# Splitting the first attention head and the GLU rows earlier, key blocks from key 0, and 128-row rotary products in a hybrid decoder layer

## What is computed

```python
proj = rmsnorm(h) @ w_in                      # u | z_s | c_q | c_kv | k_pe | z_a
ys = gelu(ssm_scan(u) + d * u)                # S5 heads
ys = ys * sigmoid(ys @ w_glu + b_glu)         # GLU
ssm_out = ys * silu(z_s)                      # 1024 rows of comb
q = rmsnorm(c_q) @ w_uq                       # 8 heads, 128 + 64 (rotary)
c, k_pe = rmsnorm(c_kv), rope(k_pe)
o = attention(q, c, k_pe, causal) @ w_uv      # prompt: per head; sample: over pages
y = concat(ssm_out, o * silu(z_a)) @ w_out    # comb, 2048 rows
out = rmsnorm(h + y)
```

## Time and profile before

| | before |
|---|---|
| median of 3 runs | 1257.17 us (1252.75 to 1259.44) |
| the profiled execution | 1260.12 us |
| its span, first to last instruction | 1258.4 us |
| PE busy | 1128.7 us (90%) |
| PE weight load busy | 1032.3 us (82%) |
| DVE busy | 585.2 us (47%) |
| ACT busy | 375.0 us (30%) |
| POOL busy | 120.8 us (10%) |
| mean granted clock of PE | 0.946 of full speed |

### The profile page before, as it was taken

The page is one execution under the profiler, slowest core; times in us unless marked ns, Lnnn a source line. Parts: engine busy times, 40 slices in busy tenths (PEclk is TensorE's granted clock), DMA queues, the critical chain, the costliest instruction groups (busy, mean ns, idle before and its releaser), DMA issues.

```text
span 1258.4 us, 25162 instructions
## 1 busy us (share of the span) xinstructions
PE 1128.7 (90%) x9906; PEld 1032.3 (82%) x9906; DVE 585.2 (47%) x1205; ACT 375.0 (30%) x622; POOL 120.8 (10%) x192
## 2 busy tenths in 40 slices
PE   3899949999999999596989997799999988999993
PEld 3799949999999999586989975566666648999992
DVE  5843513442588521384646363455555462232224
ACT  6311101111233222335422213444444351121213
POOL 0000110000000000003405301022223100000000
PEclk8799969999999999698989898899999999999996
DMA  9343491332343532415437656166777728323203
GB/s 265 85 126 102 119 145 43 86 85 85 94 125 102 143 103 82 101 47 180 126 92 218 201 179 212 34 194 194 214 213 220 203 76 266 105 67 100 84 17 135
DMA packets 197187, 165.70 MB, mean 132 GB/s; under 512 B 35195, under 2 KB 163478, under 8 KB 195270
## 3 DMA queue, kind: packets, MB, share of 16 engines
q1 hardware_dynamic: 176358, 118.08, 33.4%
q0 software_dynamic: 9696, 27.04, 8.0%
q10 hardware_dynamic: 11048, 19.41, 4.6%
HBM read 139.36 MB, written 22.78 MB: 129 GB/s over the span
## 4 chain that ended last, share of the span: by engine, by line
PE 80%; DVE 6%; DMA 5%; ACT 3%; issue 3%; SPq 1%; POOL 0%; ACTq 0%; DVEq 0%
PE gemm L1758 13%; PE gemm L1760 13%; PE gemm L1759 13%; PE gemm L2084 5%; PE gemm L2086 4%; PE gemm L2085 4%; PE misc L1997 4%; PE gemm L2037 3%; PE gemm L2016 2%; DMA w_raw<-w_out 1%; PE misc L1834 1%; PE misc L1841 1%; PE misc L1983 1%; PE misc L1785 1%; PE gemm L1947 1%
## 5 line engine op out<-in xcount | busy, mean ns | idle before, releaser
L1758 PE MATMUL gemm<-xh,w_hi 128*128 128x260 f32 (+2 forms) x1120 | 321.9, 287 | 0.2 <-DVE w_lo L1152 0.2
L1760 PE MATMUL gemm<-xh,w_lo 128*128 128x260 f32 (+2 forms) x1120 | 319.8, 286 | 0.0
L1759 PE MATMUL gemm<-xl,w_hi 128*128 128x260 f32 (+2 forms) x1120 | 319.5, 285 | 0.0
L1152 DVE TENSOR_TENSOR w_lo<-w_raw,w_hi 128x2048 fp32r<-128x2048 f32 (+3 forms) x65 | 113.6, 1748 | 259.8 <-ACT w_hi L787 258.8
L1758 PEld LDWEIGHTS gemm<-xh,w_hi 128*128 128x128 f32 x1120 | 212.2, 189 | 1.1 <-DVE w_lo L1152 0.4
L1759 PEld LDWEIGHTS gemm<-xl,w_hi 128*128 128x128 f32 x1120 | 212.3, 190 | 0.0
L1760 PEld LDWEIGHTS gemm<-xh,w_lo 128*128 128x128 f32 x1120 | 212.1, 189 | 0.0
L787 ACT ACTIVATE w_hi<-w_raw 128x2048 fp32r<-128x2048 f32 (+3 forms) x63 | 90.7, 1439 | 354.7 <-PE gemm L1760 339.4
L2084 PE MATMUL gemm<-comb_hi,w_hi 128*128 128x260 f32 x512 | 147.4, 288 | 3.9 <-DVE w_lo L1642 2.9
L2086 PE MATMUL gemm<-comb_hi,w_lo 128*128 128x260 f32 x512 | 145.4, 284 | 0.0
L2085 PE MATMUL gemm<-comb_lo,w_hi 128*128 128x260 f32 x512 | 145.4, 284 | 0.0
(11 more groups left out here) (340 smaller groups left out, 1949.1 us busy)
## 6 DMA issues: line engine op xcount, KB each, us to landing
w_raw<-w_in SPq DMA_DIRECT2D x35, 1024.0 KB, 6.0
...
z_d<-ev ACTq DMA_DIRECT2D x16, 260.0 KB, 2.1
...
```

The lines of the kernel that those rows point to most:

```text
L1152: dve.tensor_tensor(w_lo[:, slot, 0:width], w_raw[:, slot, 0:width], w_hi[:, slot, 0:width].bitcast(F32), ALU.subtract).then_inc(w_lo_read ...
L1758: pe.matmul(acc, a, xa, start=k == 0, stop=False)
L1759: pe.matmul(acc, a, xb, start=False, stop=False)
L1760: last = pe.matmul(acc, b, xa, start=False, stop=k == k_tiles - 1)
```

## The change

1. Head 0 is split during the value projection (ACT after v = 7, DVE after v = 8), `kp_lo` after v = 5, and `scores(0)` is made by PE at v = 9, ahead of the last latent transposes. An exponential of one column at v = 5 on ACT asks for its table. SP loads head 1 as soon as head 0 is split; head 1 is split at the end of tile 1. The stores of `kout` stand behind `exponential(0)` and are awaited by SP only at the end.
2. `kp_lo` gets 128 rows, the lower 64 zero.
3. The fourth tile's scores are two halves of 264 keys. Key blocks are counted from key 0, so a tile's diagonal reaches over a block's end by 16 keys of the last 16 queries; these go as a transpose of 32 rows by 16 keys (`EDGE` = 32), and the values' products start `EDGE` columns earlier from the second block on; a memset makes the rest zero.
4. GLU rows are split as they are made: low part into `comb_lo` (in place of `comb`), high part into `ghi`, stored to `g_d` in memory and loaded into `comb_hi[:, 0:8]` near the end of attention.
5. The rows of the heads are split one at a time: head 5 in tile 26, heads 0 to 2 in tile 30, 3, 4 and 6 in tile 31, 7 at the end. `gate_o` of the last head stands ahead of `sample_weights`.
6. `w_out` blocks 2 and 3 are loaded before `yt`; the half of block 1 is cut into 6, 5 and 5 k-tiles.

The diff, without semaphore renames and code that only moves:

```diff
-        EXTRA = slice(496, 512)
-        NM, SM, SME, RS, PARTS = 24, 32, 40, 48, 56
+        HALF = T_PROMPT // 2
+        NM, SM, SME, RS, PARTS, SPARE = 24, 32, 40, 48, 56, 60
+        HEADS_SPLIT = (5, 0, 1, 2, 3, 4, 6, 7)
+        SPLIT_AT = {26: (0,), 30: (1, 2, 3), 31: (4, 5, 6)}
...
-                sp.dma_start(vraw[:, u, 0:4, :], v_d[N_META:T_PROMPT, cols].rearrange("(t p) c -> p t c", p=P)).then_inc(v_loaded[u], 16)
-                sp.dma_start(vraw[0:N_META, u, 4, :], v_d[0:N_META, cols]).then_inc(v_loaded[u], 16)
+                sp.dma_start(vraw[:, u, 0:4, :], v_d[0:4 * P, cols].rearrange("(t p) c -> p t c", p=P)).then_inc(v_loaded[u], 16)
+                sp.dma_start(vraw[0:N_META, u, 4, :], v_d[4 * P:T_PROMPT, cols]).then_inc(v_loaded[u], 16)
...
+            sp.wait_ge(head_lo_done, 1)
+            load_raw(1)
+            load_rotary(1)
             sp.wait_ge(table_loaded, 16)
             sp.wait_ge(v_ready, 10)
             load_group(sp, 3)
...
-            sp.wait_ge(kpe_stored, 16 * 3)
-            sp.wait_ge(head_lo_done, 1)
-            load_raw(1)
-            load_rotary(1)
...
+            sp.wait_ge(opv_done, pages_freed(26))
+            sp.dma_start(comb_hi[:, 0:8, N_META:T].bitcast(F32), g_d.rearrange("(k p) t -> p k t", p=P)[:, :, N_META:T]).then_inc(glu_loaded, 16)
...
+            for u in range(2):
+                sp.wait_ge(w_lo_ready, B_OUT + 1 + u)
+                load_out(2 + u, u)
             sp.wait_ge(ot_ready, 2)
...
-            with sp.Fori(0, 7) as i:
+            with sp.Fori(0, 6) as i:
                 for u in range(2):
-                    sp.wait_ge(w_lo_ready, i * 2 + (B_OUT + 1 + u))
-                    load_out(i * 2 + (2 + u), u)
+                    sp.wait_ge(w_lo_ready, i * 2 + (B_OUT + 3 + u))
+                    load_out(i * 2 + (4 + u), u)
+            sp.wait_ge(kpe_stored, 16 * 3)
+            for u in range(2):
+                sp.wait_ge(glu_stored[u], 16 * 4)
...
+            def keep_high(k):
+
+                act.wait_ge(gated, k + 3)
+                if k < 2:
+                    act.wait_ge(ev_stored[k % 2], 16 * (EV_STORES[k % 2] - 8 + 1))
+                else:
+                    act.wait_ge(comb_lo_done, k - 1)
+                    act.wait_ge(glu_stored[k % 2], 16 * (k // 2))
+                act.activation(ghi[:, k % 2, N_META:T], comb[:, k, N_META:T], ACT.Copy).then_inc(comb_hi_done, 1)
+                act.wait_ge(comb_hi_done, k + 1)
+                act.dma_start(g_d[k * P:(k + 1) * P, N_META:T], ghi[:, k % 2, N_META:T].bitcast(F32)).then_inc(glu_stored[k % 2], 16)
+
...
+                if n > B_GLU:
+                    keep_high(n - B_GLU - 1)
...
+            keep_high(7)
...
+                if v == 5:
+                    act.activation(stat[:, SPARE:SPARE + 1], ident[:, 0:1], ACT.Exp)
+                if v == 7:
+                    head_hi(0)

             act.wait_ge(v_ready, 10)
...
-            head_hi(0)
-            act.wait_ge(kpe_copied, 1)
-            kv = kout[:]
-            act.dma_start(KPE_OUT[0][0:512, :].rearrange("(t p) r -> p t r", p=P), kv[:, 0:4, :]).then_inc(kpe_stored, 16)
-            act.dma_start(KPE_OUT[0][512:T_PROMPT, :], kv[0:N_META, 4, :]).then_inc(kpe_stored, 16)
...
-                    act.activation(out[:, N_META:T_PROMPT], S_BANK[1][:], ACT.Exp, scale=SCALE, bias=bias,
+                    act.activation(out[:, HALF:T_PROMPT], S_BANK[1][:, 0:HALF], ACT.Exp, scale=SCALE, bias=bias,
                                    accum_out=stat[:, SM + at_m:SM + at_m + 1])
-                    act.activation(out[:, 0:N_META], S_BANK[0][:, EXTRA], ACT.Exp, scale=SCALE, bias=bias,
+                    act.activation(out[:, 0:HALF], S_BANK[0][:, 0:HALF], ACT.Exp, scale=SCALE, bias=bias,
                                    accum_out=stat[:, SME + at_m:SME + at_m + 1]).then_inc(exp_done, 1)

...
-                tiles = min(i + 1, 3)
-                act.activation(pt[0:N_META, 0, q], TP[0:N_META, 0:P], ACT.Copy)
-                act.activation(pt[:, 1:1 + tiles, q], TP[:, P:(tiles + 1) * P].rearrange("p (j q) -> p j q", q=P), ACT.Copy).then_inc(pt_copied, 1)
+                last = act.activation(pt[:, 0:i + 1, q], TP[:, 0:(i + 1) * P].rearrange("p (j q) -> p j q", q=P), ACT.Copy)
+                if i < 3:
+                    last = act.activation(pt[0:N_META, i + 1, (i + 1) * P - EDGE:(i + 1) * P], TP[0:N_META, (i + 1) * P:(i + 1) * P + EDGE], ACT.Copy)
+                last.then_inc(pt_copied, 1)

             def copy_last_turned(m):

                 act.wait_ge(pt_ready, rounds(m) + 2)
-                act.activation(pt[:, 4, 3 * P:4 * P], TP[:, 0:P], ACT.Copy).then_inc(pt_copied, 1)
+                act.activation(pt[0:N_META, 4, 4 * P - EDGE:4 * P], TP[0:N_META, 0:EDGE], ACT.Copy).then_inc(pt_copied, 1)
...
+            def comb_high(h):
+                act.wait_ge(o_gated, h + 1)
+                if h < 5:
+                    act.wait_ge(opv_done, pages_freed(27))
+                else:
+                    act.wait_ge(kpe_stored, 16 * 3)
+                act.activation(comb_hi[:, 8 + h, OWN_COLS], comb[:, 8 + h, OWN_COLS], ACT.Copy).then_inc(comb_hi_done, 1)
...
+            act.wait_ge(kpe_copied, 1)
+            kv = kout[:]
+            act.dma_start(KPE_OUT[0][0:512, :].rearrange("(t p) r -> p t r", p=P), kv[:, 0:4, :]).then_inc(kpe_stored, 16)
+            act.dma_start(KPE_OUT[0][512:T_PROMPT, :], kv[0:N_META, 4, :]).then_inc(kpe_stored, 16)
+            act.dma_start(KPE_OUT[1], kv[N_META:N_META + N_SAMPLE, 4, :]).then_inc(kpe_stored, 16)
...
-                    if n // 4 + 1 < N_HEADS:
+                    if n and n // 4 + 1 < N_HEADS:
                         head_hi(n // 4 + 1)
                 copy_turned(n)
                 if n % 4 and n + 1 < N_TILES:
                     exponential(n + 1)
+                if n == 1:
+                    head_hi(1)
...
+                if n in SPLIT_AT:
+                    for i in SPLIT_AT[n]:
+                        comb_high(HEADS_SPLIT[i])
+
             copy_last_turned(N_TILES - 1)
             sample_exp(N_SAMPLE - 1)
-            act.wait_ge(o_gated, 7)
-            for r in (8, 10, 12, 14):
...
+            def keep_low(k):
+                dve.wait_ge(comb_hi_done, k + 1)
+                tt(comb_lo[:, k, N_META:T], comb[:, k, N_META:T], ghi[:, k % 2, N_META:T].bitcast(F32), ALU.subtract).then_inc(comb_lo_done, 1)
+
+            for n in range(B_GLU, B_GLU + 8):
+                if n == B_GLU + 4:
+                    norms()
+                glu(n, n // 2, n % 2, B_GLU if n < B_GLU + 6 else n + 2)
+                if n > B_GLU:
+                    keep_low(n - B_GLU - 1)

...
+            keep_low(7)
+            dve.wait_ge(comb_lo_done, 8)
+            for u in range(2):
+                dve.wait_ge(glu_stored[u], 16 * 4)
...
+                if v == 5:
+                    dve.memset(kp_lo[QK_ROPE:P].bitcast(F32), 0.0)
+                    dve.wait_ge(kp_hi_done, 1)
+                    tt(kp_lo[0:QK_ROPE], ev[0:QK_ROPE, 0, 0:T_PROMPT], kp_hi[0:QK_ROPE].bitcast(F32), ALU.subtract).then_inc(kp_lo_done, 1)
+                if v == 8:
+                    head_lo(0)
...
+            dve.wait_ge(c_t_ready, 6)
+            dve.tensor_copy(kout[:], misc[1][:, 0:5 * QK_ROPE].rearrange("p (t r) -> p t r", t=5)).then_inc(kpe_copied, 1)
+            for j in range(1, 4):
+                dve.memset(pt[:, j, j * P - EDGE:j * P], 0.0)
...
+                    head_lo(1)
...
+                if n == N_TILES - 1:
+                    sample_max(N_SAMPLE - 1)
+                for i in SPLIT_AT.get(n, ()):
+                    comb_low(i)
+
+            gate_o(N_HEADS - 1)
             sample_weights(N_SAMPLE - 1)
-            gate_o(N_HEADS - 1)
...
-            comb_low(slice(12, 14), OWN_COLS, 7)
-            comb_low(slice(14, 15), OWN_COLS, 8)
...
-            comb_low(slice(15, 16), OWN_COLS, 9)
+            comb_low(7)
...
+                    return pe.matmul(out, qr, kp_lo[:, keys], start=False, stop=True)
+
+                if i < 3:
+                    width = max(256, keys_of(m))
+                    last = accumulate(S_BANK[m % 2][:, 0:width], slice(0, width))
+                else:
+                    accumulate(S_BANK[1][:, 0:HALF], slice(HALF, T_PROMPT))
+                    pe.wait_ge(exp_done, m)
+                    last = accumulate(S_BANK[0][:, 0:HALF], slice(0, HALF))
+                last.then_inc(scores_ready, 1)
...
+                    if v == 9:
+                        pe.wait_ge(v_copied, 9)
+                        pe.wait_ge(kp_lo_done, 1)
+                        scores(0)
...
-                    return pe.matmul(out, qr[0:QK_ROPE], kp_lo[0:QK_ROPE, keys], start=False, stop=True)
...
-                pe.transpose(TP[0:N_META, 0:P], p[:, 0:N_META], ident[:])
-                for j in range(min(i + 1, 3)):
```

(28 more changed lines are left out.)

134 lines of the change are left out of this document (52 added, 82 removed).

## The result

The changed kernel takes 1221.15 us (median of 4 runs, 1216.37 to 1223.83); the kernel before, beside it on the same chip, 1256.33 us (1252.75 to 1259.44). The ratio is 0.9708, 95% interval 0.9684 to 0.9731. The gain is 35.2 us where 30.6 were summed up.

The account below looks back on a forecast made before the run. PE, 80% of the span, was taken as the bound, so only its work and waits count. Gains of 11.1 + 12 + 0 + 2.5 + 5.0 = 30.6 us off 1260.1, less 2.95 for the median, gave 1226.5 us, range 1215 to 1241.

Parts of the forecast that it names:

- part 1: Change from value projection to attention loop: first page scores no longer wait for head 1's load; gain 11.1 us (8 to 14).
- 2 loop: Attention loop, eight heads of four tiles: shorter PE work saves 1.5 us a head, 12 us in all (5 to 18).
- 3 GLU rows: GLU blocks: one added copy, store and subtraction each, covered by PE's products; counted as 0, 5.6 us without cover.
- 4 end of attention: End of attention: splits made earlier, wait before page weights 2.39 to 0.4 us; gain 2.5 us (0 to 4).
- 5 output: Output projection: w_out block 2 loaded before yt gives 4.4, other k-tile cut 0.6; gain 5.0 us (3 to 6).
- 0.99 + 1.04: Loop, gains a head: 0.99 us from kp_lo on 128 rows, 1.04 from the last tile's even 264-column halves.
- The values' 0.65: Loop: value products of 1408 instead of 1792 columns, taken as a gain of 0.65 us a head.
- The edges' 1.2: Loop: four added 32-row edge transposes a head at 0.30 us each, a cost of 1.2 us a head.
- The rival with 0.52 for each: Loop: 32-row transposes let PE run empty on both sides, 0.52 us each; loop gains 5, total 1233.5 us; chance 0.20.
- the slower one: Rival in the loop: 32 edge transposes at 1.45 us each bring a loss over 6.3 us; 1264 at 1.5; chance 0.03.
- the right ones: Signs: page scores near 780 us, head 1.5 us shorter, page-weight wait at most 0.5, none before output block 2, clock 1.00.
- one of the wrong ones: Sign against the forecast, in the attention loop: ACT or DVE as releasers of PE within a head.

Follow-up runs that it names:

- experiment 1: Changed kernel with the first head's moved steps put back behind the value projection, but without SyncE's wait for the kout stores: 1236.09 us.
- experiment 8: Changed kernel with head-opening value products cut around the page-weight transposes and DVE's page copy ahead of gating and the next head's split: 1212.92 us, ratio 0.9649.
- Experiment 7: Changed kernel with the splits of the first seven heads' output rows all in the last tile, 31: 1220.51 us.
- experiment 6: Changed kernel with the GLU rows' low split on 2 columns instead of 520, and the third and fourth output weights again loaded behind the residual rows: 1225.35 us.

## Why the prediction was right, and where not

By its own steps. "Measured" is from the traces, but for part 1, where it is the time of experiment 1 (15.4 by the trace).

| part | predicted | measured |
|---|---|---|
| 1 first head | 11.1 (8 to 14) | 14.9 |
| 2 loop | 12 (5 to 18) | 13.9 |
| 3 GLU rows | 0 | -0.9 |
| 4 end of attention | 2.5 (0 to 4) | 5.3 |
| 5 output | 5.0 (3 to 6) | 5.1 |
| sum | 30.6 | 38.3 |

The medians differ by 35.2. The stretches behind the first value product carry all of the sum but the GLU rows, so what is missing, 3 us, must lie ahead of it or in the executions that weren't profiled. The clock ahead of the value projection moves single executions by about as much (3.5 of the 4.7 us there), but which of the others it slowed is not known, and the 3 us stay open.

*First head.* The mechanism was right in that everything hung on the load of head 1, which stood behind head 0's late split, and in that the split of head 1 did move ahead of a page copy. One step of it was wrong: it is not "just" the kout store that holds this load. Experiment 1 leaves that wait out and the stretch is as long as before (59.4 and 59.3 us), for SyncE's queue and the traffic beside the load are next. The sizes were too careful by 3.8 us, or 4.3 by the trace. 1.4 lie on the links to the page scores, where the stores' issues overlap the exponential; 1.2 in the value projection, where the 0.6 us of scores(0) found room and the rest is a slightly faster execution and the point from which the steps count; 0.3 in the split of head 1, which costs 0.74 instead of 1.0; and 1.35 in the clock, which is low over the first page scores with this part taken back and was already back in the changed kernel's execution. The last was not in the sum at all, and it is luck: four of the kernels above have this part and take 6.3 to 6.7 us from group 0 to 1, not 5.67 (in three of them at most 0.34 of it is their own, by the product on 64 rows). The first page scores came at 773.1 us, not near 780; 4.7 us of that are the earlier start of the value projection. The table load of 1.28 us left the chain as said.

*Loop.* The total was near, its terms were not. kp_lo and the last tile were given 0.99 + 1.04 = 2.03 a head, and taken back together they cost 1.90: right, though 1.60 of it is the rotary product and only 0.48 the even split alone. The values' 0.65 were wrong: the products got 0.57 us shorter, but PE's saving ran into DVE's page copy, and experiment 8 had to reorder DVE to get at it. The edges' 1.2 were wrong the other way: some 0.1 in each tile, and part of it hidden. That the two errors partly cancel, -0.55 said and -0.16 found, is luck; it left 1.5 against 1.74. For the edges I had taken 0.30 from the row of a product of 16 columns, arguing that wider work ahead must run out first. The way in is indeed paid, at 0.1, but behind an edge of 32 columns hardly anything (0.04) is lost. The rival with 0.52 for each is refuted, and with it the slower one, which needed 1.45.

*GLU rows.* The late store cost nothing, as said, but DVE had no cover while POOL was at work. The term was put at nothing because 0.7 us a split fit beside PE's products; beside POOL's work a split took 1.84.

*End of attention.* Of the 5.3 us, 4.0 lie between the last page scores and the first output product (13.4 before, 9.4 after). Experiment 7 prices the place of the first four splits at 2.5 now, though by a wait for ACT, where the kernel before waited for DVE. The rest I have not taken apart; what could make it up is the splits of rows 0 to 7 that no longer exist there, the values, whose products are shorter here too, and the order of gating and copy. The wait for the page weights' copy fell from 2.39 us to 0.5, 0.4 said. The GLU rows' load was not waited for.

*Output.* Right in size, and in both terms: 4.5 behind the first turned block (4.4 said) and 0.5 ahead of it (0.6 said); the wait of 2.85 us is gone and the clock behind it is 1.00, 0.94 and 0.63 before. The order of the loads makes it, by experiment 6.

Of the signs named beforehand the right ones showed (the page scores even 7 us early), but so did one of the wrong ones: ACT and DVE as releasers of PE within a head, 0.5 us each. They did not overturn the sum. The wait for ACT was in the kernel before as well; the one for DVE is the values' missing gain.
